# First pieces in four buffers, the last gate product behind projection and biases, two split tiles, and the second norm inside the loop's last turn

## The reference, cut to what matters

```python
mix = hybrid_mixer(x, w_in, ...)            # z = x @ w_in, depthwise convolutions, pooling, then @ w_out
h = layer_norm(ALPHA * x + mix, ln1_g, ln1_b)
ffn = moe_ffn(h, ...)                       # 32 experts, top 4 of each token, swiglu, width 1024
ple = sigmoid(h @ ple_w_gate) * (p @ ple_w_proj)
x = layer_norm(ALPHA * h + ffn + ple, ln2_g, ln2_b)
# second block
u = rmsnorm(x, norm1_w); proj = u @ w_in_2  # then windowed attention, gated recurrence, a dense FFN
```

## Time and profile before

| | |
|---|---|
| median of 3 runs | 2074.31 us |
| the profiled execution | 2073.48 us |
| its span (first to last instruction) | 2071.6 us |
| TensorE matmul busy | 2040.2 us (98%) |
| VectorE busy | 1555.5 us (75%) |
| ScalarE busy | 1136.9 us (55%) |
| mean granted TensorE clock | 0.998 of full |

### The profile page before, as it was taken

The page is one execution under the profiler, slowest core; times in us unless marked ns, Lnnn a source line. Parts: engine busy times, 40 slices in busy tenths (PEclk is TensorE's granted clock), DMA queues, the critical chain, the costliest instruction groups (busy, mean ns, idle before and its releaser), DMA issues.

```text
span 2071.6 us, 26310 instructions
## 1 busy us (share of the span) xinstructions
PE 2040.2 (98%) x9284; PEld 1628.6 (79%) x9284; DVE 1555.5 (75%) x1435; ACT 1136.9 (55%) x1055; POOL 240.5 (12%) x249
## 2 busy tenths in 40 slices
PE   8999999999999999999999999989999999999998
PEld 5865478888888888888888888858888878888887
DVE  6987499999999999999999999985674443333333
ACT  3132277777777777777777777754114632222222
POOL 0006311111111111111121211110000000000000
PEclk9999999999999999999999999999999999999999
DMA  5233599999999999999999999941132213222321
GB/s 227 92 142 120 211 392 399 389 387 376 385 381 385 379 384 377 387 376 385 379 383 381 377 385 377 386 177 61 67 96 83 82 41 112 102 100 83 122 82 41
DMA packets 79158, 522.71 MB, mean 252 GB/s; under 512 B 10352, under 2 KB 10880, under 8 KB 22144
## 3 DMA queue, kind: packets, MB, share of 16 engines
q1 hardware_dynamic: 66496, 483.88, 59.8%
q0 software_dynamic: 9056, 30.62, 5.8%
q10 hardware_dynamic: 3552, 7.46, 1.1%
HBM read 501.31 MB, written 18.60 MB: 251 GB/s over the span
## 4 chain that ended last, share of the span: by engine, by line
PE 94%; DVE 3%; DMA 1%; issue 1%; ACT 1%; SPq 0%; DVEq 0%; ACTq 0%
PE bank L1116 26%; PE bank L1118 26%; PE bank L1117 26%; PE bank L1108 4%; PE bank L1125 1%; PE bank L1314 1%; PE bank L1463 1%; DMA ring<-in_wmoe 1%; PE bank L1265 1%; PE bank L1306 1%; PE bank L1154 1%; PE bank L1542 1%; PE bank L1523 1%; PE bank L1558 1%; PE bank L1505 0%
## 5 line engine op out<-in xcount | busy, mean ns | idle before, releaser
L1884 DVE TENSOR_TENSOR ring_r<-ring,room_r 128x2048 fp32r<-128x2048 f32 x384 | 875.3, 2294 | 76.4 <-ACT room_r L770 70.2
L770 ACT ACTIVATE room_r<-ring 128x2048 fp32r<-128x2048 f32 x384 | 736.1, 1918 | 175.5 <-PE bank L1118 165.1
L1117 PE MATMUL bank<-ring_r,room_r 128*128 128x512 f32 x1744 | 678.8, 389 | 0.0
L1116 PE MATMUL bank<-room_r 128*128 128x512 f32 x1576 | 622.9, 395 | 4.1 <-DVE ring_r L1884 3.9
L1118 PE MATMUL bank<-room_r 128*128 128x512 f32 x1568 | 611.4, 390 | 0.0
L1117 PEld LDWEIGHTS bank<-ring_r,room_r 128*128 128x128 f32 x1744 | 327.8, 188 | 69.0 <-issue 3.1
L1116 PEld LDWEIGHTS bank<-room_r 128*128 128x128 f32 x1576 | 295.9, 188 | 66.4 <-DVE ring_r L1884 5.9
L1118 PEld LDWEIGHTS bank<-room_r 128*128 128x128 f32 x1568 | 294.3, 188 | 62.7
L1116 PE MATMUL bank<-room_r,ring_r 128*128 128x512 f32 x520 | 203.5, 391 | 1.8 <-DVE ring_r L2046 0.9
L1118 PE MATMUL bank<-room_r,ring_r 128*128 128x512 f32 x512 | 199.3, 389 | 0.0
L1117 PE MATMUL bank<-ring_r 128*128 128x512 f32 x384 | 149.5, 389 | 0.0
(11 more groups left out here) (297 smaller groups left out, 2159.4 us busy)
## 6 DMA issues: line engine op xcount, KB each, us to landing
ring<-in_wmoe SPq DMA_DIRECT2D x384, 1024.0 KB, 12.7
ring<-in_wf SPq DMA_DIRECT2D x33, 1024.0 KB, 4.8
ring<-in_wd SPq DMA_DIRECT2D x7, 2048.0 KB, 9.3
ring<-in_wp SPq DMA_DIRECT2D x14, 1024.0 KB, 4.8
ring<-in_wo SPq DMA_DIRECT2D x2, 2048.0 KB, 9.3
ring<-in_wd SPq DMA_DIRECT2D x2, 1024.0 KB, 8.7
room<-in_xtok ACTq DMA_DIRECT2D x1, 2048.0 KB, 12.6
h_rows<-room POOLq DMA_DIRECT2D x4, 512.0 KB, 3.0
```

Source lines behind the costliest of these rows:

```text
L770: act.activation(w_hi[s_ % PAIRS], raw_w[ORDER[s_]], ACT.Copy)\
L1116: pe.matmul(out, x_hi, w_hi, start=start, stop=False, skip_group_check=True)
L1117: pe.matmul(out, x_hi, w_lo, start=False, stop=False, skip_group_check=True)
L1884: dve.tensor_tensor(w_lo[i], raw_w[i], w_hi[s_ % PAIRS].bitcast(F32), ALU.subtract)\
```

## The change

1. Tiles 2 and 3 of the first stage are split: their half of the first chunk is rounded on ScalarE (`w0_hi`) and subtracted on VectorE (`w0_lo`), both ahead of the split of chunk 1.
2. In block 0 the pieces s = 0, 1, 4, 5, 6, 7, 8 use buffers 0, 2, 3, 1, 2, 3, 0. The splits of s = 1 and 4 move ahead of the last gate's results on ScalarE and VectorE, with waits on `plep_ready`, `ple_evac` and `bdn_ready`.
3. TensorE does, for g = 7, projection, both biases, then the gate.
4. The second norm and the split of its turned result move into the loop's last turn on ScalarE and VectorE; on VectorE the row selection goes ahead of `half_lo(0)`.

```diff
+        w0_hi = vr(10240, 2 * KT * P).rearrange("p (k c) -> p k c", k=KT)
+        w0_lo = ring_at(HW, 2 * KT * P, ring_r).rearrange("p (k c) -> p k c", k=KT)
...
+        def pair(first, s):
+            return {1: 2, 4: 3, 5: 1}.get(s, s % PAIRS) if first else s % PAIRS
...
# scalar
+            chunk(act, 0)
+            act.activation(w0_hi, w0_raw, ACT.Copy).then_inc(s["zhi_done"], 1)
             z_hi(1)
...
                 elif s_ == 1:
+                    act.wait_ge(s["plep_ready"], 2 * TT)
+                    act.wait_ge(s["ple_evac"], 6)
+                elif s_ == 4:
+                    act.wait_ge(s["bdn_ready"], 2 * TT)
+                elif s_ == 5:
                     act.wait_ge(s["ple_evac"], 2 * TT)
-                elif s_ in (4, 5):
-                    act.wait_ge(s["used"], s_ - 3)
                 elif s_ == 6:
-                    act.wait_ge(s["plep_ready"], 2 * TT)
+                    act.wait_ge(s["used"], after(0, 1))
                 elif s_ == 7:
-                    act.wait_ge(s["bdn_ready"], 2 * TT)
+                    act.wait_ge(s["used"], after(0, 4))
...
                     split_hi(0, 0, True)
+                    split_hi(0, 1, True)
+                    split_hi(0, 4, True)
...
                         rest_act(T)
+                        second_block_rows()
# tensor
-            chunk(pe, 0)
+            pe.wait_ge(s["zlo_done"], 3)
             for j in range(2, 4):
-                first_tile(j, range(KT)).then_inc(s["z_ready"], 1)
+                at = (j % 2) * P
+                for k in range(KT):
+                    ins = product(bank[j][:, :], w0_hi[:, k, at:at + P], w0_lo[:, k, at:at + P], x_hi[:, k, :], x_lo[:, k, :],
+                                  k == 0, k == KT - 1)
+                ins.then_inc(s["z_ready"], 1)
...
             for g in range(4, 2 * TT):
-                if g < 2 * TT - 1:
-                    ple(g)
-                else:
-                    ple_gate(g)
-                    ple_proj(g)
+                ple_proj(g)
+                if g == 2 * TT - 1:
+                    bias_down(2 * g - 8)
+                    bias_down(2 * g - 7)
+                ple_gate(g)
                 if g == 2 * TT - 2:
                     gathered(0)
-                bias_down(2 * g - 8)
-                bias_down(2 * g - 7)
+                if g < 2 * TT - 1:
+                    bias_down(2 * g - 8)
+                    bias_down(2 * g - 7)
# vector
+            dve.wait_ge(s["zhi_done"], 3)
+            dve.tensor_tensor(w0_lo, w0_raw, w0_hi.bitcast(F32), ALU.subtract).then_inc(s["zlo_done"], 1)
             z_lo(1)
...
                 if g == 2 * TT - 2:
-                    split_lo(0, 0, True)
+                    split_lo(0, 0, True, True)
                 biased(2 * g - 8)
                 biased(2 * g - 7)
+                if g == 2 * TT - 2:
+                    split_lo(0, 1, True, True)
+                    split_lo(0, 4, True, True)
...
-            half_lo(0)
-            dve.wait_ge(s["late_in"], 48)
...
+            def second_block_rows():
+                dve.wait_ge(s["late_in"], 48)
+                dve.wait_ge(s["idx_kept"], T * 2)
+                step(dve.tensor_copy(token_of[0:CAP, :], idx_row[0:CAP, :]))
+                dve.tensor_scalar(token_sel[0:CAP, :], token_row[0:CAP, :], token_of[0:CAP, :], None, ALU.is_equal)\
+                   .then_inc(s["row_sel_ready"], 1)
+                half_lo(0)
+                half_lo(1)
+                combine(0)
...
                         rest_dve(T)
+                        second_block_rows()
 
             half_lo(2)
```

More of the change, by code:

```diff
@@ L840, in first_chunk @@
                 split_hi(b, 11, first)
-            split_hi(0, 1, True)
-            for s_ in range(4, 9):
+            for s_ in range(5, 9):
                 split_hi(0, s_, True)
@@ L1944, in first_chunk @@
                 activations(b, 0)
-                split_lo(b, 9, first)
-                split_lo(b, 10, first)
+                split_lo(b, 9, first, first)
+                split_lo(b, 10, first, first)
                 turned_lo(b, 0)
-                split_lo(b, 11, first)
-            split_lo(0, 1, True)
-            for s_ in range(4, 9):
-                split_lo(0, s_, True)
+                split_lo(b, 11, first, first)
+            for s_ in range(5, 9):
+                split_lo(0, s_, True, True)
             first_chunk(0, True)
@@ L2036, in _, with rest_dve @@
-            second_norm(1)
-            combine(2)
-            first_root(1).then_inc(s["x2_ready"], 1)
-            combine(3)
-            second_norm(2)
-            second_norm(3)
-            first_rms(2)
-            first_rms(3)
-            for k in range(KT):
-                dve.wait_ge(s["uT_done_a"], k + 1)
-                dve.scalar_tensor_tensor(uT_lo[k], bank[k][:, :], pcol("norm1", k), uT_hi[:, k, :].bitcast(F32),
-                                         ALU.mult, ALU.subtract).then_inc(s["uT_done_v"], 1)
+            def rest_dve(b):
+                activations(last, 1)
+                split_lo(b, 2, True)
+                turned_lo(last, 1)
+                split_lo(b, 3)
@@ new lines, in second_block_rows @@
+            def second_block_rows():
+                dve.wait_ge(s["late_in"], 48)
[6 more added lines that the diff above has]
+                combine(0)
+                second_norm(0)
+                combine(1)
+                first_root(0).then_inc(s["x2_ready"], 1)
+                second_norm(1)
+                combine(2)
+                first_root(1).then_inc(s["x2_ready"], 1)
+                combine(3)
+                second_norm(2)
+                second_norm(3)
+                first_rms(2)
+                first_rms(3)
+                for k in range(KT):
+                    dve.wait_ge(s["uT_done_a"], k + 1)
+                    dve.scalar_tensor_tensor(uT_lo[k], bank[k][:, :], pcol("norm1", k), uT_hi[:, k, :].bitcast(F32),
+                                             ALU.mult, ALU.subtract).then_inc(s["uT_done_v"], 1)
@@ L2050, in _, with more_dve @@
+            def more_dve(b):
+                with dve.If(b[0] < T):
+                    block_dve(b[0])
+                    if b[1:]:
+                        more_dve(b[1:])
+            with dve.Fori(1, BLOCKS + 1, ROUNDS) as b:
+                with dve.If(b <= T):
+                    more_dve([b + q for q in range(ROUNDS)])
+                    with dve.If(T < b + ROUNDS):
+                        rest_dve(T)
+                        second_block_rows()
             half_lo(2)
```

103 lines of the change are left out of this document (40 added, 63 removed).

## The result

The changed kernel takes 2080.28 us (median of 7 runs, 2079.69 to 2083.45), where the kernel before takes 2074.31: the ratio is 1.0031, 95% interval [1.0021, 1.0041]. That is 0.3% slower, 6 us, where I had forecast 2 us more and no change that could be told. Its profiled execution took 2080.11 us with a span of 2078.3, 6.7 us more than the span before.

A forecast was written before the change was run, and what follows sets the result against it. TensorE, its matmuls busy for 98% of the span, was taken as the bound. -0.9 (tiles), +0.9 (gate, buffers, block 1's load) and +2.0 (norm) made +2.0; with the median of before 0.83 higher, 2076.3 us, range 2072.4 to 2080.0.

The forecast's parts named there:

- a granted clock under 1 between 241 and 253: Sign of a wrong forecast: TensorE's clock drops around the last gate, ahead of block 0.
- The tiles, -0.9: First stage: two split tiles save 3.1 us of TensorE work, but the second pool matmul's wait leaves 0.9 us gained.
- tile 4 about 3 us earlier: Sign of a right forecast in the first stage: tile 4 starts about 3 us earlier, the second pool matmul less than 1.
- The last gate, +5.67: Ahead of block 0: TensorE waits for biased(4) and biased(5), so the gate and block 0 start 5.67 us later.
- The buffers, -4.4 and -0.4: Block 0's two stalls on splits go, 4.4 us; block 1's wait for a load goes, 0.4 us.
- the one of about nil: Block 0: s = 8 and the activations on VectorE are ready at about 271.8, when TensorE asks for them.
- the rival of a failed margin: Block 0: activations behind s = 8, or s = 6, come 2.5 us late and TensorE stalls; 2078.8 us, chance 0.08.
- The norm's front, -1.4: Loop's end: the row selection is done earlier, so TensorE's sums and VectorE's norm behind them come 1.4 us earlier.
- The exit behind `uT_lo`, tile 2 waits 3.4: After the loop: VectorE's 5.5 us exit delays half_lo(2); TensorE's tile 2 waits 3.4 us, net +2.0 with the front.
- The rival of a hidden exit: VectorE's queue takes its operations earlier, tile 2 doesn't wait; sum -1.4, 2072.9 us, chance 0.12.
- The clock, left at nothing: The forecast's sum held no clock loss; the wait from 241.5 to 245.2 was put just short of 4 us.
- the rival's one fall of 6.8 us: Last gate: the clock falls to half in the new wait for 6.8 us, losing 3.4; 2079.7 us, chance 0.15.

The follow-up runs named there:

- e5: The changed kernel with VectorE evacuating biased(4) and biased(5) before split_lo(0, 0) instead of behind it; 2077.53 us, ratio 1.0012 to the kernel before.
- e6: The kernel before with the four buffers and the projection ahead of the last gate, both biases still behind the gate; 2071.22 us, ratio 0.9981 to before.
- e9: The changed kernel with the ScalarE and VectorE loops ending at 35 instead of 54, one empty turn instead of seven; 2076.77 us, ratio 1.0005 to before.
- e7: The kernel before with the second norm in the loop's last turn and the exit moved behind the product of tile 3; 2073.29 us, ratio 0.9988.
- e1: The kernel before with only the two split tiles; 2075.79 us, ratio 1.0003 to before.
- e3: The kernel before with only the second norm moved into the loop's last turn; 2078.99 us, ratio 1.0017 to before.
- e4: The changed kernel with matmuls nobody reads filling its waits ahead of bias_down(6) and projection tile 2; 2078.75 us, ratio 1.0017 to the kernel before.
- e2: The kernel before with only the four buffers and the last gate behind projection and biases; 2076.71 us, ratio 1.0010 to before.
- e11: A repetition of e8 beside e10 on the same chip; 2071.20 us, ratio 0.9975 to the kernel before.
- e8: The kernel before with the two split tiles and the edits of e6 and e7 together; 2069.18 us, ratio 0.9971 to before.
- e10: e8 without the two split tiles; 2069.84 us, ratio 0.9975 to the kernel before.

## Why the prediction was wrong

The time was outside my range by 0.3 us, and on the side to which I had given 0.26. The sign that I had named for being wrong, a granted clock under 1 between 241 and 253, is in the trace. Point by point:

- **The tiles, -0.9.** The mechanism was right: TensorE stands before the second pool matmul until VectorE's pooled input ends. Between the two traces it measured -0.3, since that input ended 0.5 us later (124.58 + 0.69 = 125.27 against 124.77). But VectorE's first operation started 0.5 us later too (14.36 against 13.86), before any of the change, and counted from there the tiles give 0.8 in every trace. Right. The 3.1 us of work were somewhat too much: the 0.222 counts records that only reach into the stretch; by the starts (36.53 to 36.77 and on) a fast matmul takes 0.228, a split tile 5.5, and two tiles save 2.8. Nothing hung on it, since the wait for the input takes up the difference, but the sign "tile 4 about 3 us earlier" measured 1.9 (33.75 against 35.67, with the later data in it).
- **The last gate, +5.67.** Measured 5.9: the wait for `biased(4)` and `biased(5)`, with the cause shown by e5, and the 2.2 us bare behind the gate. Right.
- **The buffers, -4.4 and -0.4.** Measured -4.4 and -0.5; every margin held, the one of about nil as well. e6 shows them by themselves. Right, and so the rival of a failed margin is out.
- **The norm's front, -1.4.** Measured -1.5. Right.
- **The exit behind `uT_lo`, tile 2 waits 3.4.** Measured 3.8. The branches of L2068 run from 1409.8 to 1415.5, and from the end of the last `uT_hi` (1404.93 + 4.73 = 1409.66) to `half_lo(2)` at 1415.66 it is 6.0 us instead of 5.5; e9 shows that the empty turns are the cause and e7 that it costs only in this place. Right, 0.4 too small. The rival of a hidden exit is out.
- **The clock, left at nothing. This step failed.** The prediction said that "stretches of 2.2 us and less left the clock alone", took 4 us as the point from which a wait decides, saw one place only ("just short" of it, chance 0.15) and gave it 6.8 us at half clock. Each of these was wrong. The waits of 3.1 and 3.8 us each brought one fall, the second in a place for which I had worked out a bare wait of 3.4 us without asking what the clock does. Each lasted 3.4 us and not 6.8, and cost 1.7. Two falls are 3.4 us: with them my own sum, 2.0 + 3.4 = 5.4, would have given 2079.7, 0.6 under what was measured. In the two traces the clock is 3.4 of the 6.7 us; the rest of the miss, 3.3 us where I had 2.0, is made up of small terms: 0.5 for the data that came later, 0.4 for the longer exit, 0.34 for the step near 1560. That the rival's one fall of 6.8 us leads to the same 2079.7 is luck: it stood in one place, where there were two of half the length.

The figure of 2.2 us came from one execution. In the profiled execution of before the stall of 2.19 us in block 0 left the clock at 1.00, and I read this as what the clock does. The same stall stands in e1, e3 and e7, 2.15 us long, ending at 254.59, 257.09 and 256.41, and in each a stretch at half clock of 3.4 us starts behind it, at 255.2, 258.3 and 257.4. In e3:

```profile
256.00:258.00 2.00, 0.91 (x4) 0.78 (x5) 2.00 (x2) 0.95 (x1) 1.17 (x2) 1.00 1.00 377
258.00:260.00 2.00, 2.00 (x7) 1.57 (x6) 1.28 (x1) 0.00 (x0) 2.00 (x1) 0.56 0.98 369
260.00:262.00 2.00, 2.00 (x6) 1.55 (x6) 0.00 (x0) 0.28 (x1) 0.43 (x3) 0.58 1.01 410
262.00:264.00 2.00, 2.00 (x10) 1.67 (x9) 0.33 (x1) 2.00 (x2) 0.00 (x0) 1.00 1.02 416
```

The bare wait of 2.22 us ahead of block 0 brought one in e4 and e5, and none in the changed kernel, e2 and e9, where the clock had fallen about 11 us before its end. So a wait of 2 us is a risk of 1.7 us that one execution shows and the next doesn't, and the kernel before has it too. This is also why the 3.4 us of the two traces are not the share of the clock in the medians: the profiled execution of before, at a mean of 0.998, has no fall but the long one behind the sums and the one at the program's end, while the 82 runs of before beside the experiments lie at 0.9965 on average. The seven runs of the changed kernel lie at 0.9956; for before's runs on that occasion, apart from the profiled one, no clock is on record, so the share in the measured 6 us stays open. The six waits of 3.1 us and more that are new (two in the changed kernel, one each in e2, e3, e5 and e9) brought a fall each time, in e9 0.25 us before the wait's end, in the others up to 1.2 us behind it.

The Trainium skill (TensorE: Matmul & The Clock Gate, HAM oscillation) says that waits for data between bursts of matmuls can send the engine to half clock each time. The trace agrees here, for both new waits, at 1.7 us each. I had weighed that rule against one trace and given it 0.15; the trace had no wait between 2.2 and 4 us to hold against it.

## What to carry to other kernels

Where TensorE sets the time, give every new bare wait two terms: its length, and what the clock takes behind it. Here that was 1.7 us in six of six waits of 3.1 to 3.8 us, and in five of nine of 2.2 us, so one trace without a fall shows nothing; in the medians the second term is smaller, where the kernel before has such falls as well. An instruction moved ahead in one engine's order needs its inputs moved ahead in the other's: the same three ideas made the kernel 0.3% slower with `bias_down` ahead of the gate and the loop's exit behind `uT_lo`, and 0.2 to 0.3% faster (e11, e8) with the two put where nobody waits. A loop with a fixed upper bound is paid for at its exit, turn by turn, by whoever waits for the engine's next operation.

## What the runs showed of the hardware

**The stretches at half clock.** In the thirteen profiled executions, from 15 us on and apart from the last one, which the end of the program cuts off, every stretch at half clock was 3.4, 6.8 or 10.2 us long: 10.2 behind the sums in e6 and e8, 6.8 there in the others, 3.4 everywhere else. Their places move. At 1385 in e1 one of 3.4 us began behind a wait of only 1.87 us, while waits of 1.75 us in e6, e8, e10 and e11 brought none. At about 186 us in e2, e3, e4 and e7 one came where TensorE had not waited: it was at the end of 28 narrow matmuls (128x32, 3.21 us in e3), which stand at the same place in before, where the clock stayed up. By run, the mean clock explains most of the spread: of 82 runs of the kernel before, the 14 at 0.998 have a median of 2073.52 us, the 22 at 0.997 of 2074.80, the 41 at 0.996 of 2076.34, the 5 at 0.995 of 2077.11. Differences under 2 us between kernels have to be read with the clock beside them.

**Table loads moved into the loop.** With the norm in the last turn's branch, ScalarE loads a function table twice in each turn, ahead of the sigmoids (L832) and ahead of a split (L782). These groups (line, engine, operation, count, busy, mean ns, idle before) are absent before:

```profile
L832 ACT ACT_TABLE_LOAD x12 | 15.4, 1283 | 0.2
L782 ACT ACT_TABLE_LOAD x11 | 14.1, 1283 | 0.2
```

They are the 29 us more of ScalarE's busy time, 23 loads of 1.28 us. They cost nothing that shows here: TensorE's time from block 1 to the last block is the same to 0.1 us as before, and ScalarE is idle 44% of the span. e1, e2 and e6 have none of these loads, e3, e4, e5 and e9 have the same 23, and e7, e8, e10 and e11, where the branch goes on from the norm's Sqrt to the Sigmoid of the first projection results, have none. I read this as the compiled program loading tables by what the loop's body ends with, whether the branch is taken or not; that the end of the branch decides it agrees with all of these kernels, but was not tried by itself. A kernel that ScalarE bounds would pay for it in every turn.
